# Other order between the output projection and the first weighing, forget-gate levels prepared ahead with Relu on ScalarE, Tanh for the front gates

## What is computed

```
n = rms_norm(h, g1) * (1 + scale1) + shift1
ya, yb, yc = sparse attention, stick-breaking attention, gated linear attention (GLA) of n @ w_in
gates = sigmoid(n @ w_gate + b_gate)              # 3 branches x 1024
merged = gates[0]*(ya@w_oa) + gates[1]*(yb@w_ob) + gates[2]*(yc@w_oc)
h = h + gate1 * (merged @ w_out)
x2 = rms_norm(h, g2) * (1 + scale2) + shift2
per token and head (8 heads): scores of x2's query against two sets of 128 keys,
    top 16 of each, top 16 of the 16x16 sums -> 16 expert numbers, g = softmax
    act = gelu(x2 . u_tab[expert]);  y += (g * act) * v_tab[expert]
h = h + gate2 * y
```

## Time and profile before

| | |
|---|---|
| median of three runs | 2178.39 us |
| the profiled execution itself | 2180.58 us |
| its span | 2178.8 us |
| mean granted TensorE clock | 0.951 |
| busy: TensorE / VectorE / ScalarE / GpSimd | 86% / 57% / 28% / 35% |
| DMA, mean over the span | 302 GB/s, 657.4 MB |
| indirect rows | 512, 536.9 MB |
| chain that ended last | TensorE 55%, DMA 28%, VectorE 6%, ScalarE 5% |

### The profile page before, as it was taken

How to read it: one execution, slowest core, us unless ns; L and a number is a source line. 1 busy time by engine, 2 the same in 40 slices (tenths; PEclk the granted TensorE clock), 3 DMA queues, 4 the chain that set the end, 5 groups by cost and what they waited for, 6 DMA issues and landing times.

```text
span 2178.8 us, 18595 instructions
## 1 busy us (share of the span) xinstructions
PE 1871.5 (86%) x6170; PEld 1039.5 (48%) x6170; DVE 1249.7 (57%) x3004; ACT 601.6 (28%) x1384; POOL 756.3 (35%) x595
## 2 busy tenths in 40 slices
PE   4989999899679789999999987889988877777776
PEld 3433455665568756566665533444444422232222
DVE  5177412254751375666666677666666666766654
ACT  1111123375421332222222224322322222222221
POOL 1034633144000113334343344444443444444441
PEclk8979899899899889999999999999998999999999
DMA  8203113002032579999999999999999999999995
GB/s 350 88 34 154 77 78 147 18 30 87 29 129 107 202 298 420 418 417 411 418 416 406 410 384 419 419 419 420 420 419 421 419 420 419 420 420 419 420 420 247
DMA packets 87872, 657.40 MB, mean 302 GB/s; under 512 B 9680, under 2 KB 9696, under 8 KB 14432
## 3 DMA queue, kind: packets, MB, share of 16 engines
q0 software_dynamic: 73728, 536.90, 59.8%
q1 hardware_dynamic: 13888, 119.05, 13.8%
q10 hardware_dynamic: 160, 0.26, 0.1%
HBM read 653.81 MB, written 2.10 MB: 301 GB/s over the span
## 4 chain that ended last, share of the span: by engine, by line
PE 55%; DMA 28%; DVE 6%; ACT 5%; issue 4%; POOL 1%; another core or an unknown queue 0%; DVEq 0%; SPq 0%; POOLq 0%; ACTq 0%
DMA sb<-uv_table,sb 27%; PE ps L985 21%; PE ps L562 6%; PE ps L880 5%; PE ps L564 4%; PE ps L908 3%; PE ps L913 2%; PE ps L686 2%; PE ps L672 2%; PE ps L931 1%; PE ps L849 1%; POOL sb L1842 1%; PE ps L622 1%; PE ps L509 1%; PE ps L708 1%
## 5 line engine op out<-in xcount | busy, mean ns | idle before, releaser
L985 PE MATMUL ps<-sb 128*128 128x512 f32 x2048 | 950.6, 613 | 184.9 <-ACT sb L1278 181.9
L1842 POOL DMA_INDIRECT sb<-uv_table,sb x512 | 567.0, 1107 | 1028.9 <-PE ps L985 789.9
L1699 DVE CUSTOM_DVE_ANT_0 sb<-sb 128x1024 f32<-128x1024 f32 x512 | 627.4, 1226 | 468.6 <-DMA sb<-uv_table,sb 462.2
L985 PEld LDWEIGHTS ps<-sb 128*128 128x128 f32 x2048 | 385.7, 194 | 711.3 <-issue 419.1
L1278 ACT ACTIVATE sb<-sb 128x128 f32<-128x128 f32 x512 | 177.6, 394 | 558.3 <-DVE sb L1708 548.0
L1270 ACT ACTIVATE sb<-sb 128x2 f32<-128x2 f32 x256 | 51.6, 202 | 374.7 <-DVE sb L1699 374.7
L562 PE MATMUL ps<-sb 128*128 128x512 f32 x304 | 137.7, 606 | 0.0
L1788 POOL TENSOR_SCALAR sb<-sb 128x4096 f32<-128x4096 f32 x6 | 63.7, 10612 | 190.0 <-DMA sb<-w_mod 190.0
L880 PE MATMUL ps<-sb 128*128 128x256 f32 (+1 forms) x608 | 121.7, 356 | 6.4 <-DMA sb<-w_pq 5.3
L880 PEld LDWEIGHTS ps<-sb 128*128 128x128 f32 x608 | 105.4, 200 | 32.2 <-issue 16.5
L672 PE MATMUL ps<-sb 128*128 128x256 f32 x384 | 94.6, 401 | 14.4 <-ACT sb L1111 12.3
(11 more groups left out here) (249 smaller groups left out, 1827.4 us busy)
## 6 DMA issues: line engine op xcount, KB each, us to landing
sb<-w_mod SPq DMA_DIRECT2D x12, 2048.0 KB, 8.9
sb<-w_pq SPq DMA_DIRECT2D x19, 1152.0 KB, 9.8
sb<-w_merge SPq DMA_DIRECT2D x24, 768.0 KB, 7.3
sb<-w_proj SPq DMA_DIRECT2D x8, 2048.0 KB, 12.2
sb<-w_merge SPq DMA_DIRECT2D x6, 2304.0 KB, 8.8
sb<-uv_table,sb POOLq DMA_INDIRECT x512, 29.1
sb<-w_merge SPq DMA_DIRECT2D x3, 1536.0 KB, 6.5
sb<-w_out SPq DMA_DIRECT2D x4, 1024.0 KB, 8.0
```

The costliest lines, as they stand in the source:

```text
L985: mm = pe.matmul(bank(2 * (t % 2) + f), dgw[n % NDG], row_v(n)[:, T * f:T * (f + 1)], start=(i == 0), stop=(i == PH * PK - 1))
L1699: dve.tensor_tensor_reduce(out=row_u(n), in0=row_u(n), in1=n2_tm(u // PH), scale=1.0, scalar=0.0, op0=ALU.mult, op1=ALU.add, accum_out=dot ...
L1842: pool.indirect_dma_start(out=ring[PLACE[n]], out_offset=None, in_=uv_table, in_offset=bass.IndirectOffsetOnAxis(ap=experts[u % 4][:, i:i ...
```

## The change

Five things are changed.

1. **Front gates.** `gate(n)` uses Tanh(x/2) where it used Sigmoid(x). `merge(n)` takes (gate + 1) times the product, and the factor 2 is taken out by half of gate1. `half_bias` and `half_gt1` are therefore made early.
2. **GLA levels.** VectorE only writes differences (`level_spread`), for two buffers in turn and up to two levels ahead; ScalarE makes both clamps with Relu (and with scale -1) and then the exponential.
3. **Order from w_out on.** ScalarE does `shifted(0)` before `gated_output(1, 0)`, and the first scores before `gated_output(1, 1)` and `square(1)`. VectorE picks unit 0 before `residual(1)`; it does the first four dots and two pairs of weights before `normed(1)`. TensorE asks for the second norm's sum before turns 2 to 5. The first query waits tile by tile.
4. **Late merges.** One stands ahead of slot 0 instead of three, and 23 stand in slots 0 to 35 instead of 21 in slots 2 to 33. Slot 0's merge stands before row 0 is weighed, the first half of query 3 now behind the weighing of row 3.
5. **Slots.** Queries and the output pieces stand one slot later. The picks of a unit are left out in the first four rows of a unit and doubled in its last four. The weights still go in pairs.

The diff, cut to its core (also changed: the loads that belong to moved steps on SyncE's queue):

```diff
--- before.py
+++ after.py
@@ -395,22 +396,22 @@
-        QUERY_SLOT = {4 * (q - 3): q for q in range(3, 11)}
+        QUERY_SLOT = {4 * (q - 3) + 1: q for q in range(3, 11)}
+        PICK_AT = [()] * 4 + [(i,) for i in range(8)] + [(8, 9), (10, 11), (12, 13), (14, 15)]
-        EARLY_MERGES = 3
+        EARLY_MERGES = 1
-        PIECE_SLOT = {36 + p: p for p in range(4)}
+            [0, 3, 4, 7, 8, 11, 12, 15, 16, 19, 20, 22, 23, 24, 26, 27, 28, 30, 31, 32, 33, 34, 35])}
+        PIECE_SLOT = {37 + p: p for p in range(4)}
...
@@ -952,15 +955,14 @@
             score(1)
+            squares_sum(1)
             pe.wait_ge(s["ht_ready"], 2)
             score(2)
-            squares_sum(1)
-            for n in range(EARLY_MERGES):
-                merge_products(n)
+            merge_products(0)
...
@@ -1108,7 +1109,9 @@
-                act.activation(gates[n % 2], gate_at(n), ACT.Sigmoid, bias=vcol(V_BG + n)).then_inc(s["gate_ready"], 1)
+                if n == 0:
+                    act.wait_ge(s["halved"], 1)
+                act.activation(gates[n % 2], gate_at(n), ACT.Tanh, scale=0.5, bias=half_bias[:, n:n + 1]).then_inc(s["gate_ready"], 1)
@@ -1152,7 +1155,15 @@
-                act.activation(c_e, c_e, ACT.Exp, scale=1 / TAU).then_inc(s["cex_ready"], 1)
+                if lv == 0:
+                    act.activation(c_e, c_e, ACT.Exp, scale=1 / TAU).then_inc(s["cex_ready"], 1)
+                else:
+                    e = c_lev[(lv - 1) % 2]
+                    act.activation(e[:, 2 * T:4 * T], e[:, 0:2 * T], ACT.Relu).then_inc(s["crelu"], 1)
+                    act.wait_ge(s["crelu"], 2 * lv - 1)
+                    act.activation(e[:, 0:2 * T], e[:, 0:2 * T], ACT.Relu, scale=-1.0).then_inc(s["crelu"], 1)
+                    act.wait_ge(s["crelu"], 2 * lv)
+                    act.activation(e, e, ACT.Exp, scale=-1 / TAU).then_inc(s["cex_ready"], 1)
...
@@ -1240,25 +1249,20 @@
             root(0)
+            shifted(0)
             gated_output(1, 0)
-            shifted(0)
             query_out(0)
-            gated_output(1, 1)
-            square(1)
             scores_out(0)
             tokens_out(1)
+            gated_output(1, 1)
             query_out(1)
             scores_out(1)
+            square(1)
             for m in range(2, 6):
             scores_out(2)
-            half_gate(0)
-            root(1)
-            shifted(1)
-            half_gate(1)
-            half_gate(2)
@@ -1279,9 +1283,16 @@
             exponents(0)
+            for pair in range(2):
+                gelus(pair)
+                diagonals(pair)
+            root(1)
+            shifted(1)
+            act.activation(warm, cact[:, 0:1], ACT.Gelu)
+            half_gate(0)
             for slot in range(NL // GROUP):
                 u, part = divmod(slot, 4)
-                for pair in (2 * slot, 2 * slot + 1):
+                for pair in (2 * slot, 2 * slot + 1) if slot >= 1 else ():
                     gelus(pair)
...
@@ -1448,10 +1461,10 @@
-                    done(dve.tensor_tensor(merged[:, c, :], gates[n % 2], out_at(n), ALU.mult))
+                    done(dve.scalar_tensor_tensor(merged[:, c, :], gates[n % 2], 1.0, out_at(n), ALU.add, ALU.mult))
-                    dve.tensor_tensor(gated, gates[n % 2], out_at(n), ALU.mult).then_inc(s["gate_used"], 1)
+                    dve.scalar_tensor_tensor(gated, gates[n % 2], 1.0, out_at(n), ALU.add, ALU.mult).then_inc(s["gate_used"], 1)
@@ -1499,24 +1512,28 @@
+            def level_spread(lv):
+
+                w = LEVELS[lv]
+                e0 = c_lev[lv % 2][:, 0:2 * T].rearrange("p (c l) -> p c l", l=2 * w)
+                bb = c_b.rearrange("p (c l) -> p c l", l=2 * w)
+                dve.tensor_tensor(e0, bb, bb[:, :, w - 1:w].broadcast_to([P, T // w, 2 * w]), ALU.subtract)\
+                   .then_inc(s["ce_ready"], 1)
+
+            def level(lv):
+
+                dve.wait_ge(s["cex_ready"], lv + 2)
+                if lv >= 2:
+                    dve.wait_ge(s["lev_done"], lv - 1)
+                dve.tensor_tensor(c_qk[lv % 2], cqk, c_lev[lv % 2], ALU.mult).then_inc(s["cqk_ready"], 1)
+                dve.wait_ge(s["cqk_ready"], lv + 2)
+
+            level_spread(0)
+            level_spread(1)
-
-            def level(lv):
-
-                w = LEVELS[lv]
-                e0 = c_e[:, 0:2 * T].rearrange("p (c l) -> p c l", l=2 * w)
-                bb = c_b.rearrange("p (c l) -> p c l", l=2 * w)
-                done(dve.tensor_tensor(e0, bb, bb[:, :, w - 1:w].broadcast_to([P, T // w, 2 * w]), ALU.subtract))
-                done(dve.tensor_scalar(c_e[:, 2 * T:4 * T], c_e[:, 0:2 * T], -1.0, 0.0, ALU.mult, ALU.min))
-                dve.tensor_scalar(c_e[:, 0:2 * T], c_e[:, 0:2 * T], 0.0, None, ALU.min).then_inc(s["ce_ready"], 1)
-                dve.wait_ge(s["cex_ready"], lv + 2)
-                if lv >= 2:
-                    dve.wait_ge(s["lev_done"], lv - 1)
-                dve.tensor_tensor(c_qk[lv % 2], cqk, c_e, ALU.mult).then_inc(s["cqk_ready"], 1)
-                dve.wait_ge(s["cqk_ready"], lv + 2)
...
@@ -1547,6 +1566,8 @@
                     level(lv + 2)
+                if lv + 4 < len(LEVELS):
+                    level_spread(lv + 4)
                 if lv < len(LEVELS) - 1:
@@ -1724,30 +1745,28 @@
-            dve.tensor_scalar(half_bias, vcol(V_BG, NG), 0.5, None, ALU.mult)
-            dve.tensor_scalar(half_gt1, mcol(GT1, KT), 0.5, None, ALU.mult).then_inc(s["halved"], 1)
-            dve.wait_ge(s["halved"], 1)
             dve.wait_ge(s["ld_x2"], 16)
             normed(0)
+            for part in range(PK):
+                pick_part(0, part)
             residual(1)
             for part in range(PK):
-                pick_part(0, part)
+                pick_part(1, part)
+            dve.wait_ge(s["tm_out"], 2)
+            dot(0)
+            dot(1)
+            share_out(0)
+            dot(2)
+            weights(0)
+            dot(3)
+            weights(1)
             normed(1)
-            for part in range(PK):
-                pick_part(1, part)
-            half_merge(0)
             dve.wait_ge(s["hsq_summed"], 2)
             ins.then_inc(s["g2t_ready"], 1)
-            dve.wait_ge(s["tm_out"], 2)
-            for n in range(GROUP):
-                dot(n)
-            half_merge(1)
-            half_merge(2)
-            share_out(0)
-            weights(0)
+            half_merge(0)
@@ -1757,10 +1776,10 @@
-                if i % 2 == 0 and n >= GROUP:
+                if i % 2 == 0 and n > GROUP:
-                if u + 2 < NU:
-                    pick_part(u + 2, i)
+                for part in PICK_AT[i] if u + 2 < NU else ():
+                    pick_part(u + 2, part)
```

32 lines of the change are left out of this document (17 added, 15 removed).

## The result

The changed kernel takes 2154.2 us in the median of four runs (2148.4 to 2158.1) against 2178.3 for the kernel before: ratio 0.9887, interval 0.9861 to 0.9913. Timed once more beside the experiments it took 2158.8 (2154.1 to 2160.0), ratio 0.9907 [0.9894, 0.9921]. 2161 was forecast. The profiled execution took 2151.5, span 2149.7: 29.1 less than the profiled one of before, so this pair of traces is 5 us further apart than the medians (24.1).

A forecast was written before the change was run, and what follows sets the result against it. TensorE's time at the last output piece plus a constant was taken to set the end. 11.3 + 1.3 + 9.7 - 4.8 = 17.5 us less gave 2163.1, or 2161 at the median's level; 8 in 10 range 2149 to 2172.

The forecast's parts named there:

- What bounds it: Whole kernel: the end is TensorE's time at the last output piece plus a constant, while the ring is full there.
- The rival with the transfers as the bound: From the row loads on: row transfers set the end, 24 us less, 2154, floor 2140; chance 15%.
- Levels: GLA levels: TensorE becomes the bound at about 7.6 us a level; three levels take 22.8, not 30.4, 7.6 less.
- GLA entry: Levels 0 and 1, where VectorE worked in series: ScalarE sets their end, the first level's takeover comes 3.7 us earlier.
- Tanh: Front gates: 18 table loads go, only the one in the second head stands on the path, 1.3 us less.
- in the levels the loads' cover is the same idle time: GLA levels: table loads fall in time ScalarE waits anyway, so removing them there gains nothing.
- as if GLA had not shifted: From w_out to the first weighing: times were worked out on the old kernel's clock, ignoring earlier gains.
- w_out to the first weighing: Stretch from the output projection on: first weighing at 780.2, not 789.97, so 9.7 us less.
- some 10 us: Ahead of merge 1, before row 0 is weighed: TensorE has idled about this long, so the gate product takes 5.38.
- Given back: Behind the first weighing: 8.8 us more TensorE work, less 4.0 from running out of rows, so 4.8 slower (bounds 2 and 9).
- Four stops on ScalarE: Before row 0: stops like the 5.74 us "remote" one hit ScalarE's new steps, the kernel is slower, 2184; chance 5%.
- GLA at 9 us a level: GLA levels: lower TensorE clock or ScalarE's stream ties levels at 9 us, 5.9 less gain, 2167; chance 13%.

The follow-up runs named there:

- after: First profiled execution of the whole changed kernel, against the kernel without the change: 2151.5 us; median of its four runs 2154.2 us, ratio 0.9887.
- before: The kernel without any of the change; median 2178.3 us, its profiled execution 2180.58 us.
- the levels' version: The unchanged kernel with only the GLA levels' edit (look-ahead, two buffers, Relu on ScalarE), gates still Sigmoid: 2165.2 us, ratio 0.9941.
- the Tanh version: The unchanged kernel with only the front gates as Tanh, with the gate + 1 factor and early halves: 2169.8 us, ratio 0.9965.
- once more: Profiled execution of the whole changed kernel when timed again beside the experiments, nothing altered; median 2158.8 us, ratio 0.9907 to the unchanged kernel.
- the order's version: The unchanged kernel with only the new order from w_out on, the late merges and the slots: 2171.7 us, ratio 0.9977.
- the best version: The changed kernel with rows 0 to 3 weighed ahead of merge 1, plus unread matmuls in three TensorE waits: 2141.8 us, ratio 0.984.

## Why the prediction was nearly right

The forecast was 2161, and 2154.2 and 2158.8 were measured: the sign held, and so did most of the mechanisms and of the terms for the work. Wrong were the loads in the levels, put at nothing, the part of the levels' edit that got the credit, and the clock, which was kept fixed.

*What bounds it* held. The end is TensorE at the last piece plus transfers; the two were nearer to each other than I said. The rival with the transfers as the bound is out for after: between the first weighing and 1250 TensorE waits for no row, and with merge 1 put behind rows 0 to 3 the stretch grew by just TensorE's work (10.6). With 6.9 us less work for TensorE, waits for rows stood at once in its place.

*Levels* held: three levels took 30.4 in before, and 22.5 (572.02 to 594.50) in after, 7.9 less for a forecast of 7.6. The other 2.1 of the 9.9 are the clock: the first gate product took 5.80 in before and 3.72 in after, with the same wait of about 1 ahead of it. But I gave credit to the wrong half of the edit for VectorE's 1.4 per level: with the clamps left on VectorE the levels are as short. That the sum came out all the same is luck.

*GLA entry*: 3.7 forecast, 6.0 measured, of which 1.4 are the clock (below) and 4.5 the work; by the levels' version, which has 1.8 of work, more than half of that needs the loads gone as well.

*Tanh: the step that failed* is "in the levels the loads' cover is the same idle time". TensorE waits for a gate in each late level, and that gate follows the exponential through a load. The levels repeat at VectorE's rate, so the load counts once for all of them, and not never. ScalarE of before:

```profile
612.42 1.91 ACT L1155 ACTIVATE sb<-sb 128x2048 f32<-128x2048 f32 x1 [5.39 <-DVE sb L1514]
614.35 1.28 ACT L1111 ACT_TABLE_LOAD   x1
615.65 0.47 ACT L1111 ACTIVATE sb<-ps,sb 128x256 f32<-128x256 f32 x1
```

In the Tanh version the gate starts as its exponential of 604.98 to 606.89 ends:

```profile
606.80 0.46 ACT L1113 ACTIVATE sb<-ps,sb 128x256 f32<-128x256 f32 x1
```

The levels take 60.3 with Tanh alone and 61.8 before, 1.45 less. With the look-ahead the gate no longer stands behind an exponential that is late, so in after this gain is inside the levels' 7.9 and counted once.

*The clock*, which I had kept "as if GLA had not shifted", is the second failure. Ahead of GLA eight matmuls of L740 and four of L750 took 3.53 and 3.78 in before:

```profile
531.48 3.53 PE L740 MATMUL ps<-sb 128*64 128x512 f32 x8 [2.17 <-POOL sb L1817]
534.94 3.78 PE L750 MATMUL ps<-sb 16*128 16x512 f32 x4
```

In after:

```profile
526.80 2.37 PE L740 MATMUL ps<-sb 128*64 128x512 f32 x8 [2.17 <-POOL sb L1836]
529.11 1.98 PE L750 MATMUL ps<-sb 16*128 16x512 f32 x4
```

That is 3.0 us, of which 2.6 reach the path, and the third query's 2.8 come on top. Some of this goes with the edit and some does not. In all nine traces with Tanh gates the twelve matmuls ahead of GLA took 2.37 and 1.98, in the five without them 6.0 to 7.3 together; the first gate product of the levels took 3.72 in all eight traces with the look-ahead and 5.6 to 6.1 in the six without. These gains come with the edit each time, though it is not the work it takes away. The 3.0 ahead of stick-breaking and the third query (3.84 in after, 6.51 once more) differ between executions of one kernel. The Tanh version and the order's version both have the fast third query, and the whole can have it only once: that is likely part of why the parts sum to more.

*w_out to the first weighing*: 9.7 forecast, 11.0 and 8.0 measured, and step by step it came as worked out. The third query was to start 55.0 after w_out (748.6 less 693.6) and started 56.1 after it; two pairs' weights were to take 5.8 and took 5.6 (733.48 to 739.11); root and shift 8.3, taken 8.3; Gelu's load and the late gate 2.0, taken 1.9; merge 1 5.38 and 1.9, taken 5.81 and 1.90. The spread between the two traces of after is mostly one group of matmuls; the third query of the one timed once more:

```profile
731.08 6.51 PE L883 MATMUL ps<-sb 128*128 128x128 f32 x32 [1.93 <-DMA sb<-w_pq]
```

6.51 against 3.84, at a granted clock of 0.55 against 1.00, and 88.4 against 85.4 up to the first weighing. What I did not do is to ask what TensorE could do in its "some 10 us" of idling, which I had forecast: the version that weighs rows 0 to 3 there gives another 9 to 14 us by the medians and 8.3 in the traces, about as much as the whole order part (7.0 and 9.2).

*Given back*: +4.8 forecast, +3.6 and +5.8 measured. TensorE's wait of the earlier trace rows is gone, as said.

*The sum.* Of the 29.1 between the traces 17.5 were forecast. 3.0 ahead of stick-breaking and 1.2, 1.4, 2.1 and 2.8 for identical matmuls at another clock are 10.5 more; 1.1 remain for all the work's terms together. In the trace taken once more the first and the last of these are missing, and the time is 8.4 longer; 2.2 more of that lie behind the first weighing, where the traces of after with the same work differ by up to 3 us from the first piece to the end.

*Rivals.* Four stops on ScalarE didn't come; none is in the traces of after. GLA at 9 us a level didn't come either.

## What to carry to other kernels

Take a wait out of an engine's chain by preparing one step ahead before moving work to another engine: here the first alone gave the 10 us of the levels (2.1 of them by way of the clock). Where a wait of several us stands ahead of an engine that sets the end, look for work that is ready and put it in there: weighing four rows in such a wait gave about as much again as the whole new order, and the best version has it. And before comparing two traces stretch by stretch, compare the durations of identical matmuls in them: a clock that fell differently looks like a gain of whichever edit is tested. The same holds for waits: those for rows begin 19.0 us behind the end of the last piece in the version that weighs first (1246.15) and 19.4 in after (1256.33), so they are no sign that the transfers bind sooner there.
